# Encoder kernel: where weight sums are copied and added, when norm rows are loaded, and how far the down projection splits ahead

## The chip, the cores and the metric

The kernel runs on one core of one Trainium2 chip. The metric is the device time of one execution in microseconds; the time before is 1022.74 us, the median of 3 runs (1021.55 to 1024.2).

## What is computed

An encoder layer over two batches of 512 tokens with 1024 channels, in float32. After an input layer norm come windowed attention and a Fourier mixing path, an output projection, a residual layer norm, and a gated feed-forward block with a width-3 convolution. What the change touches is the end:

```python
def layer_norm(x, g, b):
    mu = mean(x); var = mean((x - mu) ** 2)
    return (x - mu) * rsqrt(var + EPS) * g + b

def conv_ffn(x, w_up, conv_w, conv_b, w_down):
    h = conv3(x @ w_up, conv_w) + conv_b          # 1024 -> 2 * 2816
    a, u = split(h, 2)
    return (gelu(a) * u) @ w_down                 # 2816 -> 1024

x = layer_norm(ALPHA * x + mix, ln1_g, ln1_b)
x = layer_norm(ALPHA * x + conv_ffn(x, w_up, conv_w, conv_b, w_down), ln2_g, ln2_b)
```

## The kernel before

Each engine has its own instruction list, written out by hand, and waits on semaphores. A float32 matmul is made of three matmuls on reduced operands: each operand is split into a high part (a copy by ACT, helper line 1862) and a low part (the difference, by DVE, helper line 1267, or 1700 where the sign turns). TensorE therefore needs ACT's and then DVE's split of each operand.

*Stages.* Input norm and projections, attention and Fourier mixing (to about 230 us), output projection and `x1` (the normed residual), up projection over 22 feature tiles `v` (about 310 to 764 us), down projection, final norm.

*Up projection.* For each tile of 128 features, SP loads `w_raw` two tiles ahead (`load_up`, two DMAs), DVE forms sums of weight blocks, both engines split, TensorE does seven products. DVE's `gate` writes `gated`, and SP's `store_gated` stores it to DRAM; behind each odd tile it also stores `gsum`, four row sums. The first 18 tiles (`PAIRED`) form 9 pairs (`QUADS`).

*Weight sums.* The down projection of these 18 tiles works on 2 x 2 blocks in seven products instead of eight (`PRODUCTS`), so it needs four sums of blocks of `w_down`, kept in `ts_scratch` in DRAM. SP copies blocks there (`start_weight_sum`, twelve copies of 768 KB, one behind each `load_up` of tiles 2 to 13); when four copies of a chunk have landed, POOL adds other blocks onto them with accumulating DMAs (`weight_row_sums`, lines 748 to 755, four for each chunk of three pairs, 768 KB each): two side by side, then a third, then a fourth, each waiting for the one before.

*Down projection.* 21 steps: three chunks of seven products (`STEPS`). Step `n` uses operand slot `n % 5`. SP's `load_step(n)` loads `ga_raw` and `db_raw` once step `n - 5` is done. ACT's `step_high` and DVE's `step_low` split them two steps ahead of TensorE. A step is four tiles (`t`) of nine matmuls, into four PSUM banks; two sets of banks alternate, so a step waits until the banks of step `n - 2` are taken. Steps 0, 2, 3 and 6 are taken by ACT (`take_step`, a copy to `part_sum`), the others by DVE (`add_step`, line 1802, added to `part_sum`).

*The first residual.* SP reloads `x1` into `acc` (eight DMAs, 512 KB each, line 589), then the norm rows `gain_bc` and `bias_bc` (lines 590, 591). ACT scales both rows after its work of step 0, and everything else of ACT is queued behind that. POOL then does `acc * gain + bias` in sixteen operations (`residual`, lines 725 and 727), and, once the last steps are taken, `acc + part_sum` in eight (line 772).

*The end.* The four unpaired feature tiles are multiplied last (`down_last`, 16 groups of 12 matmuls), from splits `last_high` and `last_low`. DVE adds each group to `acc` (`add_last`, line 1810), then statistics (1270), the centring and the scaling (1835, 1842); SP stores the result.

Of the kernel before, what the change touches and what calls it, by code (L numbers as in the profile page):

```python
# [13 lines left out]
P = 128  # L14
# [155 lines left out]
def build(nc, x_prompt, x_sample, ln_in_g, ln_in_b, rel_table, w_in, attn_sink, w_fourier, g_attn,  # L170
# [172 lines left out]
    with ExitStack() as ctx:  # L343
# [17 lines left out]
        ts_copy = [sem(f"ts_copy{c}") for c in range(QUADS // CHUNK)]  # L361
# [62 lines left out]
        def _(sp):  # L424
# [69 lines left out]

            sp.wait_ge(proj_ps, 2 * TILES)
            sp.wait_ge(ss_ps, 1)
            load_wo(0)
            sp.wait_ge(logit_done, GRP * UNITS)
# [34 lines left out]
            def start_weight_sum(j):  # L533

                c, i = divmod(j, 4)
                src = (quarter[B11], quarter[B22], b12, quarter[B21])[i]
                sp.dma_start(ts_dram[i, :, quads(c), :], src[:, quads(c), :]).then_inc(ts_copy[c], 16)

            def load_step(n):
                c, i = divmod(n, 7)  # L540
                a, w, s = PRODUCTS[i][0], PRODUCTS[i][1], n % SLOTS
                if i == 0:
                    for e in range(2):
                        sp.wait_ge(g_out[e], 32 * CHUNK * (c + 1))
                    sp.wait_ge(gs_out, 16 * CHUNK * (c + 1))
                    sp.wait_ge(ts_sum, 64 * (QUADS // CHUNK))
# [18 lines left out]
            for v in range(FT):  # L565
                if v < PLAIN:
                    sp.wait_ge(c_ps, 4 * v + 4)
                    load_up(v + 2)
                elif v + 2 < FT:
                    sp.wait_ge(p_ps[3], v + 1 - PLAIN)  # L570
                    load_up(v + 2)
                    if v - PLAIN < 12:
                        start_weight_sum(v - PLAIN)
                elif v + 2 == FT:
                    sp.wait_ge(p_ps[3], v + 1 - PLAIN)
                    sp.wait_ge(p_ps[1], FT - PLAIN)
# [13 lines left out]
            sp.dma_start(gain_bc[:], ln1_g.partition_broadcast(P)).then_inc(gb_in, 16)  # L590
            sp.dma_start(bias_bc[:], ln1_b.partition_broadcast(P)).then_inc(gb_in, 16)
# [23 lines left out]
        def _(pool):  # L615
# [126 lines left out]
            def weight_row_sums(c, part):  # L742


                k, w = [ts_dram[i, :, quads(c), :] for i in range(4)], quads(c)
                if part == 0:
                    pool.wait_ge(ts_copy[c], 64)
                    pool.dma_start(k[0], b12[:, w, :], accum_op=ALU.add).then_inc(ts_sum, 16)  # L748
                    pool.dma_start(k[2], quarter[B22][:, w, :], accum_op=ALU.add).then_inc(ts_sum, 16)
                elif part == 1:  # L750
                    pool.wait_ge(ts_sum, 64 * c + 32)
                    pool.dma_start(k[1], k[0], accum_op=ALU.add).then_inc(ts_sum, 16)
                else:
                    pool.wait_ge(ts_sum, 64 * c + 48)
                    pool.dma_start(k[3], k[1], accum_op=ALU.add).then_inc(ts_sum, 16)

            for c in range(QUADS // CHUNK):
                for part in range(3):
                    weight_row_sums(c, part)
# [5 lines left out]
            for t in range(TT):  # L765

                pool.wait_ge(x0_ready, TT + t + 1)
                if t < TB:
                    pool.wait_ge(dn_dve, taken(STEPS - 2, t)[1])
                else:  # L770
                    pool.wait_ge(dn_dve, taken(STEPS - 1, t - TB)[1])
                pool.tensor_tensor(acc[:, t, :], acc[:, t, :], part_sum[:, t, :], ALU.add).then_inc(x0_ready, 1)
# [490 lines left out]
        def _(dve):  # L1263
# [455 lines left out]
            def up_tail(v):  # L1719
# [17 lines left out]
                sum_c12(v)  # L1737
                gate(v, 0)
# [6 lines left out]
                if v + 2 < FT:  # L1745
                    low_a11(v + 2)
                    sum_c11(v + 1)
                    if v % 2 and v < PAIRED:
                        row_sums(v)
                elif v + 2 == FT:  # L1750
                    step_low(0, 0)
                    step_low(0, 1)
                else:
                    step_low(1, 1)
# [57 lines left out]
            lows = [(0, 0), (0, 1), (1, 0), (1, 1), (2, 0), (2, 1), (3, 0), (3, 1)]  # L1812
            for n in range(STEPS):
                for t in range(TB):
                    if not by_act(n):
                        add_step(n, t)
                    if t % 2 and n + 2 < STEPS:
                        step_low(n + 2, t // 2)
                    elif n + 2 == STEPS and t == 3:
                        last_low(0, 0)  # L1820
                        last_low(0, 1)
                    elif n + 1 == STEPS:
                        if t == 1:
                            for j, w in lows[2:5]:
                                last_low(j, w)
                        elif t == 3:
                            for j, w in lows[5:8]:
                                last_low(j, w)
# [30 lines left out]
        def _(act):  # L1859
# [336 lines left out]
            def up_tail(v):  # L2196
# [11 lines left out]
                centre(v, up_bank(v, 0), 1, 0)  # L2208
                gelu(v, 0)
# [11 lines left out]
                else:  # L2221
                    step_high(1, 1)
# [40 lines left out]
            for n in range(STEPS):  # L2263
                for t in range(TB):
                    if by_act(n):
                        take_step(n, t)
                    if t % 2 and n + 2 < STEPS:
                        step_high(n + 2, t // 2)
                if n == 0:
# [57 lines left out]
```

## Time and profile before

| | |
|---|---|
| time, median of 3 runs | 1022.74 us |
| profiled execution | 1024.54 us |
| its span, first to last instruction | 1022.7 us |
| TensorE matmul busy | 971.3 us, 95% |
| DVE busy | 794.6 us, 78% |
| ACT busy | 487.6 us, 48% |
| POOL busy | 243.9 us, 24% |
| mean granted clock of TensorE | 0.981 |
| DMA moved | 142.21 MB |

The profile comes from one execution. Times in the trace are microseconds from the span's start. A wait is put down to the producer whose signal ended it. PE is TensorE, SPq and POOLq are the issuing of DMAs by these engines.

### The profile page before, as it was taken

The numbers are of one execution on the slowest core, as the hardware profiler recorded it, in microseconds if no ns is written. First come the engines' busy times: TensorE is split into PE (matmuls) and PEld (weight loads), VectorE is DVE, ScalarE is ACT, GpSimd is POOL, SyncE is SP. The second block draws the span as 40 slices with busy tenths as digits, with TensorE's granted clock in tenths as the row PEclk, the third lists the DMA queues.
The fourth block names the chain that finished last, engine by engine and source line by source line (L and its number), as shares of the span: only waits on it lengthen the run. The fifth ranks groups of instructions, "written<-read, shape, count | busy, mean of one in ns | idle before, by whom it ended". The sixth has DMA issues, their size and how long they took to land. (4 is left out here: it accounts for less than half of the span.)

```text
span 1022.7 us, 12252 instructions
## 1 busy us (share of the span) xinstructions
PE 971.3 (95%) x4506; PEld 806.9 (79%) x4506; DVE 794.6 (78%) x1156; ACT 487.6 (48%) x748; POOL 243.9 (24%) x222
## 2 busy tenths in 40 slices
PE   7999999999999999999999999999998499999596
PEld 5888888998888788887888788788886388888385
DVE  6664667886776899988887887888783689776988
ACT  5574667986113755444444544544542545333000
POOL 2400336784930000001001001000000795001722
PEclk9999999999999999999999999999999699999799
DMA  8334131009032114349539639524258555754012
GB/s 301 94 99 128 42 104 42 1 3 324 15 133 92 54 52 144 134 154 226 165 115 242 168 124 232 139 93 144 83 201 319 224 195 201 244 199 158 8 62 103
DMA packets 108891, 142.21 MB, mean 139 GB/s; under 512 B 20779, under 2 KB 71935, under 8 KB 108832
## 3 DMA queue, kind: packets, MB, share of 16 engines
q1 hardware_dynamic: 104352, 129.82, 38.2%
q0 software_dynamic: 3264, 9.44, 5.3%
q10 hardware_dynamic: 1216, 2.17, 0.7%
q8 instruction: 36, 0.59, 0.2%
q14 instruction: 23, 0.19, 0.1%
HBM read 112.32 MB, written 47.97 MB: 157 GB/s over the span
## 5 line engine op out<-in xcount | busy, mean ns | idle before, releaser
L780 PE MATMUL ps<-db_hi,ga_hi 128*128 128x512 f32 x252 | 99.2, 394 | 16.9 <-DVE db_lo L1267 16.9
L781 PE MATMUL ps<-db_lo,ga_hi 128*128 128x512 f32 x252 | 98.8, 392 | 0.0
L782 PE MATMUL ps<-db_hi,ga_lo 128*128 128x512 f32 x252 | 98.8, 392 | 0.0
L780 PE MATMUL ps<-x1h,wa_hi 128*128 128x512 f32 x192 | 76.6, 399 | 6.8 <-DVE w_lo L1267 6.8
L781 PE MATMUL ps<-x1l,wa_hi 128*128 128x512 f32 x192 | 75.5, 393 | 0.0
L782 PE MATMUL ps<-x1h,w_lo 128*128 128x512 f32 x192 | 75.3, 392 | 0.0
L2159 ACT ACTIVATE hc<-U,taps 128x512 f32<-128x512 f32 x60 | 48.7, 813 | 54.1 <-DVE U L1649 41.5
L725 POOL TENSOR_TENSOR acc<-acc,gain_bc 128x1024 f32<-128x1024 f32 x12 | 37.9, 3154 | 152.9 <-ACT bias_bc L1862 152.9
L780 PEld LDWEIGHTS ps<-db_hi,ga_hi 128*128 128x128 f32 x252 | 47.8, 190 | 27.6 <-issue 17.7
L1267 DVE TENSOR_TENSOR ga_lo<-ga_raw,ga_hi 128x1536 fp32r<-128x1536 f32 x21 | 45.2, 2153 | 26.4 <-ACT ga_hi L1862 26.4
L1802 DVE TENSOR_TENSOR part_sum<-part_sum,ps 128x512 f32<-128x512 f32 x68 | 45.3, 681 | 24.6 <-PE ps L782 24.6
L2164 ACT ACTIVATE hc<-hc 128x512 f32<-128x512 f32 x44 | 27.8, 633 | 71.1 <-DVE hc L1666 71.1
L748 POOL DMA_DIRECT2D ts_scratch<-in_w_down x3 | 4.0, 1333 | 238.0 <-DMA ts_scratch<-in_w_down 238.0
L1862 ACT ACTIVATE wa_hi<-w_raw 128x1024 fp32r<-128x1024 f32 x44 | 46.4, 1062 | 26.0 <-DVE w_raw L1567 16.6
L781 PEld LDWEIGHTS ps<-db_lo,ga_hi 128*128 128x128 f32 x252 | 47.9, 190 | 10.0
L782 PEld LDWEIGHTS ps<-db_hi,ga_lo 128*128 128x128 f32 x252 | 47.8, 189 | 10.0
L1267 DVE TENSOR_TENSOR w_lo<-w_raw,wa_hi 128x512 fp32r<-128x512 f32 (+1 forms) x64 | 54.8, 884 | 0.0
L1862 ACT ACTIVATE ga_hi<-ga_raw 128x1536 fp32r<-128x1536 f32 x21 | 31.2, 1484 | 48.8 <-DMA db_raw<-in_w_down 24.2
L780 PEld LDWEIGHTS ps<-x1h,wa_hi 128*128 128x128 f32 x192 | 36.3, 189 | 15.5 <-DVE w_lo L1267 8.1
L1662 DVE SCALAR_TENSOR_TENSOR hc<-U,taps,hc 128x511 f32<-128x511 f32 x60 | 43.2, 748 | 5.7 <-ACT hc L2159 5.7
L1862 ACT ACTIVATE U<-ps 128x512 f32<-128x512 f32 x60 | 35.5, 591 | 24.9 <-PE ps L782 24.9
L634 POOL TENSOR_TENSOR rstd<-ve,half_neg 128x1 f32<-128x1 f32 x20 | 22.2, 1112 | 94.0 <-DVE ve L1280 94.0
(318 smaller groups left out, 2961.9 us busy)
## 6 DMA issues: line engine op xcount, KB each, us to landing
w_raw<-in_w_up SPq DMA_DIRECT2D x44, 512.0 KB, 5.2
ga_raw<-gs_scratch SPq DMA_DIRECT2D x21, 768.0 KB, 4.7
gs_scratch<-gsum SPq DMA_DIRECT2D x9, 1024.0 KB, 4.7
ts_scratch<-in_w_down SPq DMA_DIRECT2D x12, 768.0 KB, 6.9
db_raw<-ts_scratch SPq DMA_DIRECT2D x12, 768.0 KB, 6.1
db_raw<-in_w_down SPq DMA_DIRECT2D x9, 768.0 KB, 6.8
gs_scratch<-gated SPq DMA_DIRECT2D x9, 512.0 KB
ts_scratch<-in_w_down POOLq DMA_DIRECT2D x6, 768.0 KB, 12.3
```

Source lines behind the costliest of these rows:

```text
L634: pool.tensor_tensor(rstd[:, t:t + 1], ve[:, t:t + 1], half_neg[:, 0:1], ALU.pow).then_inc(rstd_ready, 1)
L725: chain.mark(pool.tensor_tensor(dst, dst, gain_bc[:], ALU.mult))
L748: pool.dma_start(k[0], b12[:, w, :], accum_op=ALU.add).then_inc(ts_sum, 16)
L780: pe.matmul(out, whi, xhi, start=start, stop=False, skip_group_check=onto)
L781: pe.matmul(out, whi, xlo, start=False, stop=False, skip_group_check=onto)
L782: return pe.matmul(out, wlo, xhi, start=False, stop=stop, skip_group_check=onto)
L1267: dve.tensor_tensor(out, full, f32(hi), ALU.subtract).then_inc(done, 1)
L1662: chain.mark(dve.scalar_tensor_tensor(out=hc[:, part, b, 1:SEQ], in0=src[:, 0:SEQ - 1], scalar=tap(v, part, 0), in1=hc[:, part, b, 1:SEQ], ...
L1802: dve.tensor_tensor(dst, dst, ps[:, DOWN_BANKS[n % 2][t], :], ALU.add if sign > 0 else ALU.subtract).then_inc(dn_dve, 1)
L1862: ins = act.activation(out, in_, ACT.Copy, scale=scale) if scale != 1.0 else act.activation(out, in_, ACT.Copy)
L2159: act.activation(hc[:, part, b, :], src, ACT.Identity, bias=taps[:, 1, col + 2 * FT:col + 2 * FT + 1], scale=taps[:, 0, col + 2 * FT:col + ...
L2164: act.activation(hc[:, 0, b, :], hc[:, 0, b, :], ACT.Gelu).then_inc(gelu_done, 1)
```

## The change

The edits, in the order of the diff:

- `ts_copy` becomes one semaphore. SP issues all twelve copies in the attention stage, behind `load_wo(0)` and ahead of its wait for the logits, and none in the up projection.
- POOL's accumulating DMAs become 36 of 256 KB: for each pair two behind the gates of its even tile and two, one after the other, behind those of its odd tile (`g_ready`).
- SP loads `gain_bc` and `bias_bc` for the first residual in the last tile of the up projection, behind `load_step(2)`, ahead of the last store and of the `x1` loads. ACT scales them after its splits of step 1's loop pass, not of step 0's.
- Splits of the down projection run three steps ahead; the second half of step 1 is split before the last gates and gelus.
- Steps 14 to 20 add straight into `acc`, on DVE. POOL adds the `part_sum` of the first two chunks to `acc` in sixteen half-width operations as soon as each quarter is complete (steps 8, 11, 12, 13). DVE's adds of steps 14 to 20 wait for these; its `add_last` waits for DVE's own adds only.
- The splits of the last four tiles are spread over steps 18 to 20.

```diff
@@ SP, attention stage
             load_wo(0)
+            for j in range(4 * (QUADS // CHUNK)):
+                start_weight_sum(j)
             sp.wait_ge(logit_done, GRP * UNITS)
@@ SP, up projection
                     load_up(v + 2)
-                    if v - PLAIN < 12:
-                        start_weight_sum(v - PLAIN)
...
                     load_step(2)
+                    sp.wait_ge(gs_out, 16 * QUADS)
+                    sp.dma_start(gain_bc[:], ln1_g.partition_broadcast(P)).then_inc(gb_in, 16)
+                    sp.dma_start(bias_bc[:], ln1_b.partition_broadcast(P)).then_inc(gb_in, 16)
                 store_gated(v)
...
                 sp.dma_start(acc[:, t, :], x1_dram[t]).then_inc(x_in[t], 16)
-            sp.dma_start(gain_bc[:], ln1_g.partition_broadcast(P)).then_inc(gb_in, 16)
-            sp.dma_start(bias_bc[:], ln1_b.partition_broadcast(P)).then_inc(gb_in, 16)
@@ POOL
+            def weight_row_sums(v):
+                q, k = v // 2, [ts_dram[i, :, v // 2, :] for i in range(4)]
+                pool.wait_ge(g_ready, 2 * v + 2)
+                if v % 2 == 0:
+                    pool.dma_start(k[0], b12[:, q, :], accum_op=ALU.add).then_inc(ts_sum, 16)
+                    pool.dma_start(k[2], quarter[B22][:, q, :], accum_op=ALU.add).then_inc(ts_sum, 16)
+                else:
+                    pool.wait_ge(ts_sum, 64 * q + 32)
                     pool.dma_start(k[1], k[0], accum_op=ALU.add).then_inc(ts_sum, 16)
+                    pool.wait_ge(ts_sum, 64 * q + 48)
                     pool.dma_start(k[3], k[1], accum_op=ALU.add).then_inc(ts_sum, 16)
...
-            for t in range(TT):
-                pool.wait_ge(x0_ready, TT + t + 1)
...
-                pool.tensor_tensor(acc[:, t, :], acc[:, t, :], part_sum[:, t, :], ALU.add).then_inc(x0_ready, 1)
+            for n in (8, 11, 12, 13):
+                first, half, _ = TARGETS[n - 7]
+                cols = slice(half * 512, half * 512 + 512)
+                for t in range(TB):
+                    pool.wait_ge(x0_ready, TT + first + t + 1)
+                    pool.wait_ge(dn_dve, taken(n, t)[1])
+                    pool.tensor_tensor(acc[:, first + t, cols], acc[:, first + t, cols], part_sum[:, first + t, cols], ALU.add).then_inc(x0_ready, 1)
@@ DVE (ACT's lists change in the same way)
                 sum_c12(v)
+                if v + 1 == FT:
+                    step_low(1, 1)
                 gate(v, 0)
...
-                dst = part_sum[:, first + t, half * 512:(half + 1) * 512]
+                dst = (part_sum if n < 14 else acc)[:, first + t, half * 512:(half + 1) * 512]
...
+                if n >= 14:
+                    dve.wait_ge(x0_ready, 2 * TT + {(0, 0): 0, (4, 1): 4, (0, 1): 8, (4, 0): 12}[first, half] + t + 1)
...
-                if half == 0:
-                    dve.wait_ge(x0_ready, 2 * TT + t + 1)
+                if t < TB:
+                    dve.wait_ge(dn_dve, taken((15, 19)[half], t)[1])
+                else:
+                    dve.wait_ge(dn_dve, taken((20, 18)[half], t - TB)[1])
...
+            lows = {(18, 1): (0,), (18, 3): (1,), (19, 1): (2,), (19, 3): (3, 4), (20, 1): (5, 6), (20, 2): (7,)}
             for n in range(STEPS):
                 for t in range(TB):
                     if not by_act(n):
                         add_step(n, t)
...
+                    if n == 0:
+                        step_low(2 + t // 2, t % 2)
+                    elif t % 2 and n + 3 < STEPS:
+                        step_low(n + 3, t // 2)
+                    for k in lows.get((n, t), ()):
+                        last_low(k // 2, k % 2)
@@ ACT
-                if n == 0:
+                if n == 1:
                     act.wait_ge(gb_in, 64)
                     copy(gain_bc[:], gain_bc[:], gb_ready, ALPHA)
```

## Rows read from the trace of the kernel before

**Rows 1.** Waits of TensorE, all: line, releaser, us in total, times, longest.
```profile
PE ps L780 <- DVE db_lo L1267: 16.9, 2, 15.9
PE ps L780 <- DVE d_lo L1267: 11.6, 3, 5.2
PE ps L780 <- DVE w_lo L1267: 6.8, 3, 2.4
```
**Rows 2.** Timeline of SP's DMA issues, down stage: start, duration, line, tile.
```profile
841.22 0.32 SPq L549 DMA_DIRECT2D ga_raw<-gs_scratch  x1
...
849.38 0.32 SPq L549 DMA_DIRECT2D ga_raw<-gs_scratch  x1
```
**Rows 3.** Busy time by stretch: PE, PEld, DVE, ACT, POOL; granted clock, DMA share, GB/s.
```profile
772.60:806.20 33.60, 16.72 (x73) 13.46 (x73) 12.29 (x10) 13.29 (x15) 7.86 (x3) 0.81 1.02 395
...
976.40:1022.70 46.30, 37.99 (x168) 31.14 (x166) 42.46 (x64) 0.00 (x0) 11.64 (x8) 0.96 0.23 91
```
**Rows 4.** Timelines of PE and ACT around the first stall; brackets: idle before, releaser.
```profile
806.21 0.77 PE L780 MATMUL ps<-db_hi,ga_hi 128*128 128x512 f32 x1 [15.90 <-DVE db_lo L1267]
...
796.18 1.06 ACT L1862 ACTIVATE gain_bc<-gain_bc 128x1024 f32<-128x1024 f32 x1 [19.72 <-DMA bias_bc<-in_ln_b]
```
**Rows 5.** Timelines of PE, ACT, POOL and DVE around the second stall.
```profile
961.30 0.79 PE L780 MATMUL ps<-d_hi,g_hi 128*128 128x512 f32 x1 [5.20 <-DVE d_lo L1267]
...
949.81 1.04 ACT L1862 ACTIVATE d_hi<-d_raw 128x1024 fp32r<-128x1024 f32 x1
...
942.24 10.44 POOL L772 TENSOR_TENSOR acc<-acc,part_sum 128x1024 f32<-128x1024 f32 x4 [85.00 <-DVE part_sum L1802]
...
950.36 3.41 DVE L1267 TENSOR_TENSOR d_lo<-d_raw,d_hi 128x1024 fp32r<-128x1024 f32 x1
...
961.17 1.21 DVE L1267 TENSOR_TENSOR g_lo<-g_raw,g_hi 128x1024 fp32r<-128x1024 f32 x1
...
976.35 0.69 DVE L1810 TENSOR_TENSOR acc<-ps,acc 128x512 f32<-128x512 f32 x1 [2.15 <-PE ps L782]
```
**Rows 6.** Busy time by stretch, up projection; columns as in rows 3.
```profile
480.00:500.00 20.00, 17.66 (x71) 14.09 (x71) 15.52 (x21) 8.84 (x11) 0.81 (x1) 0.91 0.73 178
500.00:520.00 20.00, 20.00 (x90) 16.57 (x89) 17.74 (x25) 9.08 (x12) 0.00 (x0) 1.00 0.55 185
```
**Rows 7.** Landing of w_raw: loads issued from 453 us, and from 472 us.
```profile
DMA to landing us min/median/max: 4.1/4.7/5.3
...
DMA to landing us min/median/max: 7.6/8.2/8.9
```
**Rows 8.** Timelines of POOL's accumulating DMAs and of SP's issues, same place.
```profile
487.45 0.81 POOL L755 DMA_DIRECT2D ts_scratch<-ts_scratch  x1 [8.30 <-DMA ts_scratch<-ts_scratch]
...
462.28 0.40 SPq L529 DMA_DIRECT2D gs_scratch<-gated  x1
...
472.32 2.58 SPq L513 DMA_DIRECT2D w_raw<-in_w_up  x2
```
**Rows 9.** Waits of SP's queue: the one for the logits in the attention stage.
```profile
SPq L493 <- DVE negm L1470: 63.1, 1, 63.1
```
**Rows 10.** Busy time by stretch, attention stage and behind it; columns as in rows 3.
```profile
170.00:180.00 10.00, 9.71 (x65) 8.81 (x65) 7.93 (x26) 8.96 (x27) 7.42 (x13) 1.00 0.01 2
...
230.00:240.00 10.00, 10.00 (x53) 8.44 (x52) 5.16 (x9) 5.40 (x10) 4.45 (x8) 1.00 1.04 316
```
**Rows 11.** Issue of load 5's second half on SP, and its landing.
```profile
783.43 1.05 SPq L551 DMA_DIRECT2D db_raw<-in_w_down  x1
...
DMA to landing us min/median/max: 16.6/16.6/16.6
```
**Rows 12.** Timeline of DVE: low parts beside POOL with adds between, back to back, alone.
```profile
803.35 2.72 DVE L1267 TENSOR_TENSOR db_lo<-db_raw,db_hi 128x1536 fp32r<-128x1536 f32 x1
...
809.83 3.95 DVE L1700 SCALAR_TENSOR_TENSOR db_lo<-db_raw,db_hi 128x1536 fp32r<-128x1536 f32 x1
...
839.15 1.80 DVE L1267 TENSOR_TENSOR ga_lo<-ga_raw,ga_hi 128x1536 fp32r<-128x1536 f32 x1 [2.07 <-ACT ga_hi L1862]
```

More of the change, by code:

```diff
@@ L360, in build @@
         gs_sum, ts_sum = sem("gs_sum"), sem("ts_sum")
-        ts_copy = [sem(f"ts_copy{c}") for c in range(QUADS // CHUNK)]
+        ts_copy = sem("ts_copy")
         step_in = [sem(f"step_in{s}") for s in range(SLOTS)]
@@ L493, in load_wo, with start_weight_sum @@
                         sp.dma_start(wor[p][kv * HD:(kv + 1) * HD], rows).then_inc(wo_in[p], 16)
+            def start_weight_sum(j):
+                c, i = divmod(j, 4)
+                src = (quarter[B11], quarter[B22], b12, quarter[B21])[i]
+                sp.dma_start(ts_dram[i, :, quads(c), :], src[:, quads(c), :]).then_inc(ts_copy, 16)
             sp.wait_ge(proj_ps, 2 * TILES)
@@ L531, in store_gated @@
                     sp.dma_start(gs_dram[S1:S4 + 1, :, q, :].rearrange("i p n -> p i n"), gsum[:]).then_inc(gs_out, 16)
[L533 to L537, printed above, removed]
             def load_step(n):
@@ L545, in load_step @@
                     sp.wait_ge(gs_out, 16 * CHUNK * (c + 1))
-                    sp.wait_ge(ts_sum, 64 * (QUADS // CHUNK))
+                    sp.wait_ge(ts_sum, 64 * QUADS)
                 if n >= SLOTS:
@@ L740, in _ @@
                 ln_rstd(t, TT)
[L742 to L751, printed above, removed]
+            def weight_row_sums(v):
[6 more added lines that the diff above has]
+                    pool.wait_ge(ts_sum, 64 * q + 32)
                     pool.dma_start(k[1], k[0], accum_op=ALU.add).then_inc(ts_sum, 16)
-                else:
-                    pool.wait_ge(ts_sum, 64 * c + 48)
+                    pool.wait_ge(ts_sum, 64 * q + 48)
                     pool.dma_start(k[3], k[1], accum_op=ALU.add).then_inc(ts_sum, 16)
-            for c in range(QUADS // CHUNK):
-                for part in range(3):
-                    weight_row_sums(c, part)
+            pool.wait_ge(ts_copy, 64 * (QUADS // CHUNK))
+            for v in range(PAIRED):
+                weight_row_sums(v)
             pool.wait_ge(gb_ready, 3)
@@ L764, in _ @@
                 residual(acc[:, t, :])
-            for t in range(TT):
-                pool.wait_ge(x0_ready, TT + t + 1)
[L768 to L771, printed above, removed]
-                pool.tensor_tensor(acc[:, t, :], acc[:, t, :], part_sum[:, t, :], ALU.add).then_inc(x0_ready, 1)
+            for n in (8, 11, 12, 13):
[5 more added lines that the diff above has]
+                    pool.tensor_tensor(acc[:, first + t, cols], acc[:, first + t, cols], part_sum[:, first + t, cols], ALU.add).then_inc(x0_ready, 1)
             for t in range(TT):
@@ L1752, in up_tail @@
                     step_low(0, 1)
-                else:
-                    step_low(1, 1)
             for j in range(4):
@@ L1807, in add_last @@
                 dve.wait_ge(dn_ps, 4 * STEPS + i + 1)
-                if half == 0:
-                    dve.wait_ge(x0_ready, 2 * TT + t + 1)
+                if t < TB:
+                    dve.wait_ge(dn_dve, taken((15, 19)[half], t)[1])
+                else:
+                    dve.wait_ge(dn_dve, taken((20, 18)[half], t - TB)[1])
                 dve.tensor_tensor(acc[:, t, cols], ps[:, last_bank(i), :], acc[:, t, cols], ALU.add).then_inc(dn_dve, 1)
-            lows = [(0, 0), (0, 1), (1, 0), (1, 1), (2, 0), (2, 1), (3, 0), (3, 1)]
+            lows = {(18, 1): (0,), (18, 3): (1,), (19, 1): (2,), (19, 3): (3, 4), (20, 1): (5, 6), (20, 2): (7,)}
             for n in range(STEPS):
@@ L1816, in _ @@
                         add_step(n, t)
[L1817 to L1828, printed above, removed]
+                    if n == 0:
[4 more added lines that the diff above has]
+                        last_low(k // 2, k % 2)
             def pieces(t):
@@ L2208, in up_tail @@
                 centre(v, up_bank(v, 0), 1, 0)
+                if v + 1 == FT:
+                    step_high(1, 1)
                 gelu(v, 0)
@@ L2220, in up_tail @@
                     step_high(0, 1)
-                else:
-                    step_high(1, 1)
             for k in range(3):
@@ L2266, in _ @@
                         take_step(n, t)
-                    if t % 2 and n + 2 < STEPS:
-                        step_high(n + 2, t // 2)
-                if n == 0:
+                    if n == 0:
+                        step_high(2 + t // 2, t % 2)
+                    elif t % 2 and n + 3 < STEPS:
+                        step_high(n + 3, t // 2)
+                if n == 1:
                     act.wait_ge(gb_in, 64)
```

## The prediction

> **What bounds the kernel now.** I read TensorE's waits first: it is busy 95% of the span, so what can be won is where it stands still. Three producers hold it up for 35.3 us: `db_lo` (16.9), `d_lo` (11.6) and `w_lo` (6.8) [rows 1]. Each is DVE's second half of an operand split, late for a reason of its own. To price them I compare what TensorE would have taken. In the down projection the loads go out at the end of a step, and two issues in a row stand 8.16 us apart [rows 2]; a step is 36 matmuls, so one costs 0.2267 us at full clock.
>
> *First stall.* TensorE stands 15.90 us before step 3 [rows 4], in a stretch with 0.81 of full clock, full DMA engines (share 1.02) and 395 GB/s [rows 3]. The cause is on ACT: it waits 19.72 us for the norm row `bias_bc`, and only then takes up the work behind it, which includes step 3's splits [rows 4]. The norm rows are queued on SP behind eight 512 KB loads of `x1`.
>
> *Second stall.* Before the last four feature blocks TensorE waits three times for `d_lo`, 5.20 us the longest. A last split of 1.21 us alone takes 3.41 on DVE while POOL adds `part_sum` to `acc` [rows 5]. Behind it DVE sets the pace to the end: in 976.40 to 1022.70 it is busy 42.46 of 46.30 us, TensorE 37.99 [rows 3].
>
> *Third.* In the up projection three stalls of up to 2.4 us [rows 1] stand where `w_raw` took 8.2 us to land and not 4.7 [rows 7], because POOL's 768 KB accumulating DMAs are in the way.
>
> **The change part by part.**
>
> *A. Small accumulates.* The first of three such places has 71 matmuls in 20 us against 90 in its neighbour [rows 6]; the other two have 78 and 79. That is 19 + 12 + 11 = 42 matmuls, 9.5 us. The load landed 3.5 us later and the stall was at most 2.4, so some 1.1 us of slack covers each `w_raw`. Now a piece has a third of the bytes and starts when `gated` is done, which SP's store shows at 462.28; the next `w_raw` load is issued at 472.32, 10.0 us later. A wide accumulate took 8.3 us of waiting and 0.8 of issue, 9.1 [rows 8]; by bytes a piece takes 3.0. An odd tile has two in series, 6.1 us, beside 1.57 MB of stores (4.0 us at the 395 GB/s of rows 3): 10.1 if nothing overlaps, the size of the gap, with 1.1 of slack behind it. An even tile has two side by side and a smaller store. I take the whole 9.5 us as won; bounds 4 and 9.5. The Trainium skill (DMA: Bandwidth & Descriptors, "Anatomy of one DMA" and "Bandwidth") gives a DMA that POOL issues some 2.0 us fixed plus bytes / 436e3 us, and advises 1 MiB or more, which speaks against 36 small ones. By it a piece is estimated at 2.6 us and the pair at 5.2, which changes little; but it makes a wide one 3.8 us where the trace has 9.1, so a fixed part could be larger too (rival 4).
>
> *B. Copies in the attention stage.* SP waits 63.1 us there for the logits [rows 9], and the copies go in ahead of that wait. One is 0.79 MB; at the 316 GB/s of a full queue [rows 10] that is 2.5 us, and twelve are 30, so they are through in half of SP's wait and the `wo` loads behind it aren't late. The DMA share there is 0.01. That a full queue disturbs nobody is seen a little later, where the share is 1.04 and TensorE busy 10.00 of 10 us [rows 10]. Cost 0; bounds 0 and 3. The copies' old places show no stall of their own, so nothing is won there.
>
> *C. Norm rows sooner, and ACT's order.* The rows are now issued behind load 2 and ahead of the last store and the `x1` loads; they land some ten us before ACT asks. Then the 15.9 us wait is gone, and I ask what is late next. I write the order out by hand with step 0 starting at 0 (764.40 in the old trace; loads, splits and steps in us from there). Step 1's `db_lo` is split ahead of the last gates: ACT is idle there, DVE is not, so the last gate, its store and loads 3 and 4 move back by 1.5, and in return the 1.0 us before step 1 (16.9 less 15.9 [rows 1]) goes. Load 3 lands at 16.6 and load 4 at 20.5. Load 5 landed at 783.43 + 16.6 = 800.0 [rows 11], 35.6 after the start; less 2.6 for the 1.05 MB of norm rows that were ahead of it, plus 1.5, it lands at 34.5. ACT, with 1.47 a split, has step 3 by 20.0, step 4 by 23.4, the norm rows by 25.3, step 2's first two banks by 26.4. It then waits for load 5, has its first half at 36.0 and empties the third bank by 36.6. TensorE wants that bank at 4.5 steps, 36.7: it just goes through. Step 5 starts at 40.8. Its two low parts on DVE come back to back beside POOL's residual. Such a split took 3.95, one with adds around it 2.72, and one with POOL out of the way 1.80 [rows 12]. From 36.0, a first one of 1.8 to 3.95 and a second of 3.95 end at 41.8 to 43.9, so step 5 starts 1.0 to 3.1 us late; step 6 has the same pair close behind and may lose 1 more. I take 3.0 us of new stall, bounds 0.5 and 6. The Trainium skill (SBUF — State Buffer, on the shared port pair) says that DVE and GpSimd take an exclusive lock for a whole instruction; by that rule, the trace agrees: beside POOL the split costs 2.15 us more.
>
> Steps 0 to 20 took from 764.40 to 955.4 (961.30 less the wait of 5.20 and three matmuls of 0.23 [rows 5]), 191.0 us, where 21 x 8.16 = 171.4 would do. Of the 19.6 us between, 19.6 - 3.0 = 16.6 are won.
>
> *D. Last splits ahead, third chunk straight into `acc`.* Behind step 17 no step split is left for DVE, so steps 18 to 20 hold the adds (0.69 each) and eight last splits (1.21 each). The latest high part comes from ACT at 949.81 + 1.04 [rows 5], 3.6 us into step 20. The last `d_lo` is placed behind the third add of step 20, about 8.0 into it, and ends at 9.2; TensorE wants it at 8.16 + 9 x 0.2267 = 10.2. POOL's eight wide adds (2.6 us each, 10.44 for four [rows 5]) become sixteen half ones behind steps 8 to 13. POOL is through with the residual at about 25 + 16 x 3.8 = 86 and needs about 1.4 for each half add; DVE's new wait on it begins with step 14 at about 118, behind which DVE's splits of step 17 and all later adds are queued, and isn't late. So the second add into `acc` comes 24 matmuls and 0.3 us after step 20, at 955.4 + 5.4 + 0.3 = 961.1 instead of 976.35 [rows 5]: 15.2 us won; bounds 11 (a pair of splits late) and 15.2. The 46.3 us behind it stay.
>
> **Sum.** 9.5 + 16.6 + 15.2 = 41.3 us. The profiled execution's span 1022.7 becomes 981.4 and its time 1024.54 becomes 983.2. That time is 1.8 above the median of the runs, 1022.74, which becomes 981.4. Forecast 982.
>
> **Rivals.**
> 1. *The wait becomes one for load 5.* 4.2 MB of `x1` are still ahead of it, and ACT, three ahead, now stands before it with step 2's banks not yet emptied. For: the margin above is 0.1 us. A load that is 4 us late costs 4, and some 2 more by the low clock (the first place in A lost 4.3 us with a wait of 2.4): 988. Against: less is ahead of it than before. Chance 0.19; 985 to 991.
> 2. *The accumulates still meet `w_raw`* in a few tiles. Then A gives nothing: 991. Against: the 10 us gap. Chance 0.10.
> 3. *The tail keeps its waits* as DVE or POOL runs late after step 5 and never catches up; D gives nothing: 997. Against: with POOL done, splits take 1.8 us again and a step leaves DVE idle. Chance 0.04.
> 4. *Slower than before.* An accumulate's 9.1 us is fixed and not by bytes. Two in series from 462.5 then run to 480.7, and every `w_raw` load from 472.3 meets one. At 4.3 us a tile, 18 tiles lose 77: 981.4 + 9.5 + 77 = 1068. It decides from the 8th such tile on, as (41.3 - 9.5) / 4.3 = 7.4. Against: nothing at all of a 768 KB transfer would have to depend on its size. Chance 0.03, and 0.01 for a milder one that just cancels the gain.
> 5. *It doesn't do what it says:* the norm rows gate ACT as before: 998. Against: they are issued before the `x1` loads in the code. Chance 0.03.
>
> **How the numbers follow.** The forecast case has 0.60, with a range of its own of 977 to 986. The range takes in rivals 1 and 2 and the bounds of A to D: 976 to 993. About 0.3%, 3 us, is what a measurement of this kernel can tell from no change. Faster 0.96, within 0.3% 0.01, slower 0.03.
>
> **What the new profile should show.** No `db_lo` wait over 4 us; if there is one it stands before step 4's third tile or at step 5. ACT's longest wait in the down stage is for load 5. No `d_lo` wait, and no `acc` add of POOL after step 14. `w_raw` lands in under 6.5 us in all tiles, and every 20 us of the up stage have 88 to 90 matmuls. A DMA share near 1 for some 30 us in the attention stage, with TensorE as busy as before. A `w_lo` wait at every second tile would prove me wrong on A, a stall before the last blocks on D, and one over 6 us at steps 3 to 7 on C.

## The result and the profile after

The changed kernel takes 982.37 us (median of 4 runs, 981.47 to 983.99); the kernel before took 1022.16 in the runs beside it. The ratio is 0.9609, with a 95% interval of 0.9589 to 0.9629: 40.0 us less, between 37.9 and 42.0. The forecast was 982, its range 976 to 993.

The profiled execution took 981.47 us with a span of 979.6. The first four waits of TensorE after the change (line, releaser, us in total, times, longest):

```profile
PE ps L786 <- DMA rows_a<-in_ln_in_b: 4.9, 1, 4.9
PE ps L781 <- DVE db_lo L1268: 1.0, 1, 1.0
PE ps L804 <- ACT acc L1872: 1.0, 1, 1.0
PE ps L781 <- ACT part_sum L1861: 0.3, 1, 0.3
```

Of the three producers in rows 1, `d_lo` and `w_lo` are gone and `db_lo` has 1.0 us left of 16.9; with the `part_sum` wait 1.3 us remain. What was there at the kernel's start (4.9) is there still. The busy time by stretch answers rows 6 and, behind the dots, rows 10, the two stretches in which the copies run:

```profile
480.00:500.00 20.00, 20.00 (x90) 16.58 (x89) 16.47 (x24) 10.71 (x14) 1.90 (x3) 1.00 0.41 93
...
170.00:180.00 10.00, 9.75 (x66) 8.82 (x64) 7.92 (x25) 9.00 (x26) 8.11 (x15) 1.00 1.00 331
180.00:190.00 10.00, 10.00 (x61) 9.21 (x60) 8.70 (x24) 8.73 (x24) 7.55 (x13) 1.00 1.03 334
```

The up projection has its 90 matmuls in 20 us, and the attention stage runs beside a full queue (share 1.00 and 1.03) as it did beside an empty one: 66 matmuls and 9.75 us where rows 10 have 65 and 9.71. The down stage, timelines of ACT and TensorE:

```profile
778.05 1.04 ACT L1861 ACTIVATE gain_bc<-gain_bc 128x1024 f32<-128x1024 f32 x1
...
789.45 1.49 ACT L1861 ACTIVATE ga_hi<-ga_raw 128x1536 fp32r<-128x1536 f32 x1 [8.45 <-DMA db_raw<-in_w_down]
...
791.48 0.51 PE L781 MATMUL ps<-db_hi,ga_hi 128*128 128x512 f32 x1 [0.32 <-ACT part_sum L1861]
796.87 0.47 PE L781 MATMUL ps<-db_hi,ga_hi 128*128 128x512 f32 x1 [0.98 <-DVE db_lo L1268]
```

ACT takes up the norm rows without waiting (rows 4: 19.72 us), and its longest wait there, 8.45 us, is now for load 5. The end, timelines of POOL and DVE, which answer rows 5:

```profile
854.47 26.00 POOL L773 TENSOR_TENSOR acc<-acc,part_sum 128x512 f32<-128x512 f32 x12 [5.32 <-DVE part_sum L1805]
...
927.26 1.22 DVE L1268 TENSOR_TENSOR d_lo<-d_raw,d_hi 128x1024 fp32r<-128x1024 f32 x1
...
930.65 0.69 DVE L1815 TENSOR_TENSOR acc<-ps,acc 128x512 f32<-128x512 f32 x1 [1.57 <-issue]
...
933.31 0.69 DVE L1815 TENSOR_TENSOR acc<-ps,acc 128x512 f32<-128x512 f32 x1 [1.24 <-PE ps L783]
```

POOL's adds end at 880.5 and the last split takes 1.22 us alone.

**Where the 43.1 us of span went.** The first matmul of step 0, TensorE's timeline:

```profile
754.27 0.39 PE L781 MATMUL ps<-db_hi,ga_hi 128*128 128x512 f32 x1
```

Step 0 starts at 754.3 where it started at 764.4: 10.1 us. Step 20 ends at 927.7 (930.65 less twelve matmuls and 0.3), so the 21 steps take 173.4 instead of 191.0: 17.6. From there to the second add into `acc` it is 5.6 us instead of 20.9: 15.3. The tail behind it is 46.3 as before. The span shrank by more than the 40.0 us of the ratio: the profiled execution before stood 1.8 us above its kernel's median, the one after 0.9 below.

### The profile page after: what moved, and what is told of

The parts are those of the page before. It is cut to its first block, busy times and chain, and to the rows that moved or that the text cites. A ratio compares the mean times of both kernels' runs of the same rounds, so it can differ in the third digit from the quotient of the medians.

```text
span 979.6 us, 12310 instructions
## 1 busy us (share of the span) xinstructions
PE 963.2 (98%) x4506; PEld 803.8 (82%) x4506; DVE 788.2 (80%) x1156; ACT 488.4 (50%) x748; POOL 275.3 (28%) x254
## 4 chain that ended last, share of the span: by engine, by line
PE 88%; DVE 6%; DMA 2%; ACT 2%; issue 2%; POOL 0%; DVEq 0%; SPq 0%; ACTq 0%; POOLq 0%
PE ps L781 28%; PE ps L783 28%; PE ps L782 28%; DMA db_raw<-in_w_down 2%; DVE bn L1271 1%; DVE acc L1834 1%; PE ps L995 1%; DVE acc L1815 1%; PE ps L1124 1%; DVE prob L1471 1%; DVE pTl L1268 1%; ACT prob L2038 1%; PE ps L816 1%; ACT pTh L1861 0%; DMA acc<-in_x_prompt 0%
## 5 line engine op out<-in xcount | busy, mean ns | idle before, releaser
L726 POOL TENSOR_TENSOR acc<-acc,gain_bc 128x1024 f32<-128x1024 f32 x12 | 37.9, 3160 | 83.8 <-ACT bias_bc L1861 83.8
L1268 DVE TENSOR_TENSOR ga_lo<-ga_raw,ga_hi 128x1536 fp32r<-128x1536 f32 x21 | 47.9, 2283 | 16.7 <-ACT ga_hi L1861 16.7
L753 POOL DMA_DIRECT2D ts_scratch<-ts_scratch x9 | 7.3, 811 | 155.3 <-DVE gated L1677 155.3
L749 POOL DMA_DIRECT2D ts_scratch<-in_w_down x9 | 7.6, 842 | 142.8 <-DVE gated L1679 142.8
L1663 DVE SCALAR_TENSOR_TENSOR hc<-U,taps,hc 128x511 f32<-128x511 f32 x60 | 43.1, 746 | 5.5 <-ACT hc L2158 5.5
L1667 DVE SCALAR_TENSOR_TENSOR hc<-U,taps,hc 128x511 f32<-128x511 f32 x60 | 43.3, 749 | 1.4
```

The costliest lines, as they stand in the source:

```text
L726: chain.mark(pool.tensor_tensor(dst, dst, gain_bc[:], ALU.mult))
L1268: dve.tensor_tensor(out, full, f32(hi), ALU.subtract).then_inc(done, 1)
L1663: chain.mark(dve.scalar_tensor_tensor(out=hc[:, part, b, 1:SEQ], in0=src[:, 0:SEQ - 1], scalar=tap(v, part, 0), in1=hc[:, part, b, 1:SEQ], ...
L1667: dve.scalar_tensor_tensor(out=hc[:, part, b, 0:SEQ - 1], in0=src[:, 1:SEQ], scalar=tap(v, part, 1), in1=hc[:, part, b, 0:SEQ - 1], op0=AL ...
```

## Experiments

Differences to the changed kernel are differences of the ratios to the kernel before, times 1022.7. Each ratio has an interval of about 0.2 points to either side, so a difference is good to some 3 us; smaller ones rest on the waits. The profiled executions give a second measure, from the first matmul of step 0 to the end of the span: 258.3 us before, 225.3 in the changed kernel; e1 238.8, e3 242.4, e4 226.6, e5 228.9, e7 228.2, e8 234.5, e9 244.3, e10 223.4, e11 241.4, e12 229.7. It leaves out the stages ahead, which scatter: with the new sums step 0 starts anywhere from 754.3 to 755.7 us. It is one execution of each kernel, and is called the down time below.

**e1, the norm rows put back.**

```diff
-                    sp.wait_ge(gs_out, 16 * QUADS)
-                    sp.dma_start(gain_bc[:], ...)      # and bias_bc, in the last tile
...
                 sp.dma_start(acc[:, t, :], x1_dram[t]).then_inc(x_in[t], 16)
+            sp.dma_start(gain_bc[:], ...)              # and bias_bc
...
-                if n == 1:
+                if n == 0:
                     act.wait_ge(gb_in, 64)
```

> The changed kernel with the norm rows put back behind the x1 loads and ACT's scaling of them back at the end of step 0's pass; the splits stay three steps ahead. Theory (the rows gate ACT, but with three steps ahead step 3's splits are already done when ACT stops, so the stall is at step 4 and smaller): rows land about 33 us after the start of step 0, step 4's splits end about 40 to 42 where TensorE wants them at 32.7; with the low clock behind it the time is 9 to 11 us over the changed kernel's 982.4, 991 to 994. Rival (the place of the rows is the whole cure, depth nothing): the old stall of 16 to 18 us is back, 998 to 1001. Rival (the depth alone covers the wait): 982 to 984.

Measured 994.19 us, ratio 0.9707 (0.9691 to 0.9724): 10.0 us more (13.5 in the down time). The size is the theory's, the place isn't. Timelines of TensorE, ACT and DVE:

```profile
795.98 0.80 PE L780 MATMUL ps<-db_hi,ga_hi 128*128 128x512 f32 x1 [12.54 <-DVE part_sum L1804]
...
789.28 1.06 ACT L1860 ACTIVATE gain_bc<-gain_bc 128x1024 f32<-128x1024 f32 x1 [13.94 <-DMA bias_bc<-in_ln_b]
...
792.69 2.65 DVE L1267 TENSOR_TENSOR ga_lo<-ga_raw,ga_hi 128x1536 fp32r<-128x1536 f32 x1 [14.36 <-ACT ga_hi L1860]
795.25 1.27 DVE L1804 TENSOR_TENSOR part_sum<-part_sum,ps 128x512 f32<-128x512 f32 x2
```

TensorE doesn't wait for step 4's splits but for a bank, in the middle of step 3: DVE's list has step 4's first low part ahead of the adds that empty step 1's last two banks. ACT stops for the norm rows, DVE for ACT's high part, and TensorE for the add queued behind it. Both lists run in order, so here the late load reached TensorE through a bank before it could through an operand.

**e9, the norm rows put back and splits two steps ahead.** The edits are those of e1 and e4 together.

> The changed kernel with both the norm rows put back (SP's place and ACT's place) and the splits two steps ahead. Alone the rows cost 0.98 points of the time and the depth 0.04. Theory (with two ahead ACT's stop lies in front of step 3's splits, so the whole old stall is back; with three ahead it only lay in front of step 4's): a db_lo wait of 14 to 16 us before step 3, 15 to 18 us over the changed kernel, a ratio of 0.976 to 0.979 to the kernel before. Rival (the two parts simply add up): 10 to 11 us, a ratio of 0.971 to 0.972.

Measured 1002.00 us, ratio 0.9781 (0.9759 to 0.9804): 17.6 us more (18.9 in the down time). The time is the theory's, the wait is longer than it said, 18.8 us, and it is the old one, for `db_lo` before step 3:

```profile
798.70 0.76 PE L780 MATMUL ps<-db_hi,ga_hi 128*128 128x512 f32 x1 [18.80 <-DVE db_lo L1267]
```

The parts do not add up (10.0 and 0.4 would be 10.4): depth is worth nothing that can be measured once the rows are early, and some 7 us while they are late (5.4 in the down time, 18.9 less 13.5).

**e4, splits two steps ahead.**

```diff
-                    if n == 0:
-                        step_low(2 + t // 2, t % 2)
-                    elif t % 2 and n + 3 < STEPS:
-                        step_low(n + 3, t // 2)
+                    if t % 2 and n + 2 < STEPS:
+                        step_low(n + 2, t // 2)        # ACT's step_high alike
...
-            lows = {(18, 1): (0,), (18, 3): (1,), (19, 1): (2,), ...}
+            lows = {(18, 3): (0, 1), (19, 1): (2,), ...}
```

> The changed kernel with splits two steps ahead again in steps 0 to 20 (the two last splits of step 18 come behind its fourth tile so that the order of signals holds). Theory (once the norm rows are out of the way, the limit at steps 4 and 5 is the landing of load 5 and DVE beside POOL, which the depth does not move): 0 to 2 us more, 982 to 985. Rival (the depth is what carries TensorE over the full queue): 8 us more or worse, over 990.

Measured 984.24 us, ratio 0.9613 (0.9596 to 0.9630): 0.4 us more, no difference that can be measured. The waits show a small one:

```profile
798.52 0.47 PE L781 MATMUL ps<-db_hi,ga_hi 128*128 128x512 f32 x1 [3.05 <-DVE db_lo L1268]
```

It is 3.05 us before step 5 against 1.3 in two waits, and the down time is 1.3 us longer. The third step of depth buys at most 1.8 us here.

**e5, only SP's loads of the norm rows put back behind `x1`;** ACT scales them at the end of step 1's pass.

> The changed kernel with only SP's two norm row loads put back behind the x1 loads; ACT still scales them at the end of step 1's pass. This puts 1.05 MB more ahead of load 5 and makes ACT wait for the rows until about 33 us after the start of step 0, just before it empties step 2's banks. Theory (a margin of nothing at step 4, so each us that load 5 is late costs about one us): load 5 lands 2.6 us later, TensorE's waits in steps 4 to 6 rise from 1.3 us to 4 to 6, 3 to 5 us more than the changed kernel, 985 to 988, and up to 2 more if the clock falls. Rival (there is slack that I did not see): 982 to 983.

Measured 985.89 us, ratio 0.9628 (0.9608 to 0.9649): 1.9 us more by the ratios, within the scatter of the 3 to 5 expected; the span of the profiled run is 4.3 longer (983.9), its down time 3.6. TensorE waits 3.3 us, in one piece. Step 0 starts at 755.0 there, so the wait, from 787.8 on, is at the first tile of step 4, for the first bank of step 2. Timelines of TensorE and ACT:

```profile
791.04 0.50 PE L780 MATMUL ps<-db_hi,ga_hi 128*128 128x512 f32 x1 [3.27 <-ACT part_sum L1860]
...
788.51 1.06 ACT L1860 ACTIVATE gain_bc<-gain_bc 128x1024 f32<-128x1024 f32 x1 [9.95 <-DMA bias_bc<-in_ln_b]
```

The size is near the theory's, the mechanism isn't. Load 5 does come some 2 us later (ACT takes it up at 792.47, 37.5 after the start of step 0, against 35.2), but TensorE already stands by then: ACT has waited for `bias_bc` with step 2's banks still full. By the time that ACT has load 5's first half and empties the third bank (793.86), TensorE is late enough not to wait for it. So the run says nothing on the slack for load 5; e10 does. What it shows is the price of the rows alone: the same late rows cost 2 to 4 us when ACT asks for them behind step 4's splits, and 17.6 in front of step 3's (e9). Of the 3.6, 2.0 are waits and about 1.6 the clock: in the 4 us behind the wait TensorE has a granted clock of 0.61 and 11 matmuls, where 17 to 19 are usual.

**e10, load 5 ahead of the eight `x1` loads.**

```diff
+            load_step(5)
             for t in range(TT):
                 sp.dma_start(acc[:, t, :], x1_dram[t]).then_inc(x_in[t], 16)
-            for n in range(SLOTS, STEPS):
+            for n in range(SLOTS + 1, STEPS):
```

> The changed kernel with the loads of step 5 issued ahead of the eight x1 loads, nothing else. Theory (load 5 behind 4.2 MB of x1 is what is left of the stall): load 5 lands some 10 us sooner, TensorE's two waits in steps 4 to 6, 1.3 us in all, go; 1 us less than the changed kernel, a ratio of 0.959 to 0.961, hardly to be told from none by the time, so the waits decide. Rival (DVE beside POOL makes the wait, whenever the load lands): a db_lo wait of 1 us or more stays or moves to step 6.

Measured 980.41 us, ratio 0.9573 (0.9553 to 0.9593). TensorE has no wait left between 175 us and the end. Its waits, all but the last two (0.3 us or less):

```profile
PE ps L787 <- DMA rows_a<-in_ln_in_b: 4.9, 1, 4.9
PE ps L805 <- ACT acc L1873: 1.3, 2, 0.9
PE ps L846 <- ACT xh L1894: 0.3, 1, 0.3
```

Load 5 was what was left of the stall: with it early, DVE's low parts of steps 5 and 6 take 3.6 to 4.0 us beside POOL, and nobody waits for them. The down time is 2.0 us shorter and leaves 171.4 us for the 21 steps, their time at full clock. The rest of the ratio's difference (0.36 points, 3.7 us) isn't shown, as the intervals overlap. Its runs are 980.16 to 980.89, the lowest median of all kernels tried.

**e11, the kernel before with only the norm rows moved.** The edits are those of e1 read backwards, on the kernel before; the new loads stand in the same place as in the change.

> The kernel before with only the norm rows moved as in the change (SP's loads in the last tile of the up projection, ACT's scaling at the end of step 1's pass); splits two steps ahead, sums and tail as before. Theory (this part alone cures the first stall and leaves the other two): the wait before step 3 goes, 1 to 3.5 us of db_lo waits appear at steps 4 to 6, w_lo (6.8) and d_lo (11.6) stay; 14 to 17 us less, a ratio of 0.983 to 0.986 to the kernel before. Rival (the depth was needed too): under 10 us, a ratio over 0.990.

Measured 1005.81 us, ratio 0.9823 (0.9798 to 0.9848): 18.1 us less than before, a little over the 14 to 17 expected, and 16.9 less in the down time. The other two producers are as in rows 1:

```profile
PE ps L781 <- DVE d_lo L1268: 11.7, 3, 5.2
PE ps L781 <- DVE w_lo L1268: 6.0, 3, 2.1
...
PE ps L781 <- DVE db_lo L1268: 1.5, 2, 1.1
```

Two moved loads and one moved pair of copies are worth nearly half of the whole change. What I had priced too high are the new waits, 1 to 3.5 us at steps 4 to 6: here they are 0.4 (the other 1.1 is the old one before step 1). With an interval of 2.6 us to either side the ratio doesn't tell 18.1 from 17.

**e3, the tail put back.** The third chunk into `part_sum`, POOL's eight wide adds behind it, the last splits behind steps 19 and 20.

```diff
-                dst = (part_sum if n < 14 else acc)[:, first + t, half * 512:(half + 1) * 512]
+                dst = part_sum[:, first + t, half * 512:(half + 1) * 512]
...
-            lows = {(18, 1): (0,), (18, 3): (1,), (19, 1): (2,), (19, 3): (3, 4), (20, 1): (5, 6), (20, 2): (7,)}
+            lows = {(19, 3): (0, 1), (20, 1): (2, 3, 4), (20, 3): (5, 6, 7)}
```

> The changed kernel with the third chunk into part_sum, POOL's eight wide adds at the end and the last splits where they were. Theory: three d_lo waits of 11 to 12 us in all and low clock behind them, 15.2 us more, 996 to 999. Rival (the tail gained in the change because DVE arrived less behind at step 18, not by this part): under 8 us more, below 990.

Measured 999.40 us, ratio 0.9760 (0.9745 to 0.9775): 15.4 us more (17.0 in the down time), with 11.4 us of `d_lo` waits. The next two kernels divide it.

**e7, only the places of the last splits put back** (the second edit of e3), POOL's adds early.

> The changed kernel with only the last splits put back to their old places (two behind step 19, three and three in step 20); POOL's adds stay early. Theory (POOL's port use made most of the second stall): uncontended splits of 1.21 us end 13.5 us after the start of step 20 where the last is wanted at 10.2; 3 to 5 us more, 985 to 988. Rival (the places alone made the stall): 12 us or more, over 994.

Measured 986.25 us, ratio 0.9632 (0.9611 to 0.9653): 2.4 us more (2.8 in the down time), just under the 3 to 5 expected and within the scatter. Two short waits:

```profile
930.88 0.50 PE L781 MATMUL ps<-d_hi,g_hi 128*128 128x512 f32 x1 [1.08 <-DVE d_lo L1268]
933.15 0.50 PE L781 MATMUL ps<-d_hi,g_hi 128*128 128x512 f32 x1 [1.31 <-DVE d_lo L1268]
```

**e8, only POOL's adds late** (the first edit of e3 and the adds that belong to it), the splits in their new places.

> The changed kernel with the last splits in their new places but the third chunk into part_sum and POOL's eight wide adds at the end as before. Theory: the splits of steps 19 and 20 take about 3.3 us each beside POOL, the last ends about 18.8 us into step 20 where it is wanted at 10.2, with low clock behind it 9 to 11 us more, 991 to 994. Rival (the new places are enough): 982 to 984.

Measured 993.70 us, ratio 0.9701 (0.9680 to 0.9722): 9.4 us more (9.2 in the down time). TensorE, DVE and POOL:

```profile
932.54 0.50 PE L782 MATMUL ps<-d_hi,g_hi 128*128 128x512 f32 x1 [2.01 <-DVE d_lo L1269]
937.57 0.80 PE L782 MATMUL ps<-d_hi,g_hi 128*128 128x512 f32 x1 [4.08 <-DVE d_lo L1269]
...
932.40 3.38 DVE L1269 TENSOR_TENSOR g_lo<-g_raw,g_hi 128x1024 fp32r<-128x1024 f32 x1
935.71 0.67 DVE L1804 TENSOR_TENSOR part_sum<-part_sum,ps 128x512 f32<-128x512 f32 x1
936.31 1.21 DVE L1269 TENSOR_TENSOR d_lo<-d_raw,d_hi 128x1024 fp32r<-128x1024 f32 x1
...
931.36 3.35 POOL L774 TENSOR_TENSOR acc<-acc,part_sum 128x1024 f32<-128x1024 f32 x1
936.53 3.22 POOL L774 TENSOR_TENSOR acc<-acc,part_sum 128x1024 f32<-128x1024 f32 x1 [1.82 <-DVE part_sum L1804]
```

POOL's part is the larger, some three to four times. A split of this size takes 3.38 us when it starts while an add of POOL is running (932.40, the add ends at 934.71), and 1.21 when POOL is idle as it starts (936.31); POOL's next add, begun at 936.53 during that split, is then the one that takes longer, 3.22 us against 2.3 for the add behind it. An add from PSUM takes 0.67 in both places. The two undone singly make 11.8 of the 15.4 us (12.0 of 17.0 in the down time); the rest shows only with both undone, or is scatter.

**e2, the weight sums put back.** Twelve copies behind the loads of tiles 2 to 13, accumulates of 768 KB.

```diff
             load_wo(0)
-            for j in range(4 * (QUADS // CHUNK)):
-                start_weight_sum(j)
...
                     load_up(v + 2)
+                    if v - PLAIN < 12:
+                        start_weight_sum(v - PLAIN)
```

> The changed kernel with the weight sums as before: twelve copies behind the loads of tiles 2 to 13, accumulates of 768 KB. Theory (these DMAs delay three w_raw loads, and nothing else hangs on them): three w_lo waits of 2.0 to 2.4 us in the up projection, 9.5 us more than the changed kernel, 991 to 993. Rival (those stalls were made by something else in the stage and the copies are free): 982 to 984.

Measured 992.01 us, ratio 0.9687 (0.9671 to 0.9704): 8.0 us more, 10.4 in the span. Three `w_lo` waits of 3.04, 1.40 and 2.06 us, 6.5 in all; step 0 starts 10.9 us later.

**e6, early copies, wide accumulates** behind the gates of tiles 5, 9 and 13.

```diff
-                pool.wait_ge(g_ready, 2 * v + 2)
+                if part == 0:
+                    pool.wait_ge(g_ready, 8 * c + 12)
+                    pool.dma_start(k[0], b12[:, w, :], accum_op=ALU.add)    # w: three pairs at once
```

> The changed kernel with the copies early, in the attention stage, but with accumulates of 768 KB, started behind the gates of tiles 5, 9 and 13, where they ran before. Theory (the size of the accumulates delays w_raw, not the copies): the three w_lo waits are back, w_raw lands in 7.5 to 9 us there, 7 to 9.5 us more, 989 to 992. Rival (the copies in the same queue did it, or needed to be there too): no wait or under 1 us each, 982 to 984.

Measured 989.60 us, ratio 0.9663 (0.9643 to 0.9682): 5.5 us more, less than the 7 to 9.5 expected, though step 0 starts 7.1 us later. The three waits are back, and `w_raw` lands late again behind tile 5. Waits, then that landing:

```profile
PE ps L783 <- DVE w_lo L1270: 5.9, 3, 2.5
...
DMA to landing us min/median/max: 8.0/8.5/9.0
```

The copies were out of the queue and it didn't help: the accumulates, wide as they are, make the waits. What the copies add to them, 2.5 us by the ratios, is within the scatter.

**e12, small accumulates, late copies.** POOL waits for a chunk's four copies before its first piece.

```diff
+                if v % 6 == 0:
+                    pool.wait_ge(ts_copy[v // 6], 64)
                 pool.wait_ge(g_ready, 2 * v + 2)
```

> The changed kernel with the small accumulates kept but the twelve copies back behind the loads of tiles 2 to 13; POOL waits for the four copies of a chunk before the chunk's first piece. The first pair's pieces can't start before about 461 us then, and twelve of them (two side by side and two in series for each of three pairs, about 5.4 us each) run on end for some 50 us, over two or three w_raw loads. Theory (what hurts is how many bytes of accumulate are ahead of a load: one piece is 1.5 to 3 us of queue where about 1.1 us of slack stands, a wide one or two are 4 and more): w_raw lands in up to 6 to 7.5 us, a few w_lo waits of under 1.3 us each, 0 to 3 us over the changed kernel, a ratio of 0.961 to 0.964. Rival (any accumulate beside a load makes the full stall, and only the pacing by the gates saved the changed kernel): w_lo waits of 2 us or more at several tiles, 8 us or more, a ratio over 0.968.

Measured 990.12 us, ratio 0.9656 (0.9615 to 0.9696), 4.8 us more: between the two, and a wide interval. The waits speak for neither as written. In the profiled execution, the slowest of the four (994.98), step 0 starts 9.2 us later than in the changed kernel, which is between the 7.1 of e6 and the 10.9 of e2; its down time is 4.4 us longer too, with a `db_lo` wait of 2.88 us and a `part_sum` wait of 1.26, and why is open. Timelines of TensorE and POOL; then the landing of the two halves of `w_raw` issued at 472.8, and of those issued at 491.8:

```profile
505.00 0.50 PE L782 MATMUL ps<-x1h,wa_hi 128*128 128x512 f32 x1 [2.35 <-DVE w_lo L1269]
565.78 0.50 PE L782 MATMUL ps<-x1h,wa_hi 128*128 128x512 f32 x1 [1.77 <-DVE w_lo L1269]
...
470.52 0.81 POOL L755 DMA_DIRECT2D ts_scratch<-ts_scratch  x1 [6.62 <-DMA ts_scratch<-in_w_down]
474.86 0.81 POOL L757 DMA_DIRECT2D ts_scratch<-ts_scratch  x1 [3.53 <-DMA ts_scratch<-ts_scratch]
...
491.54 1.13 POOL L751 DMA_DIRECT2D ts_scratch<-in_w_down  x1
492.07 1.44 POOL L752 DMA_DIRECT2D ts_scratch<-in_w_down  x1
...
DMA to landing us min/median/max: 5.0/5.5/6.1
...
DMA to landing us min/median/max: 5.1/7.0/8.9
```

The load at 472.8 has one single piece just ahead of it and lands in at most 6.1 us, without a wait. The load at 491.8 meets a single one (issued at 491.0) and the pair above: its first half lands in 5.1 us, its second in 8.9, and TensorE stands 2.35 us, as long as beside a wide one (2.50 in e6, where the halves land in 8.0 and 9.0). So a third of the bytes isn't enough: small pieces bunched around a load made a wait of the full length at two tiles. The change needs both, pieces that fit the gap (e6) and their start behind the gates, which puts them there (e12); the early copies make that pacing possible. A copy behind a load does no harm by itself: the loads issued at 434.7, 453.7 and 515.1 each have one behind them and no piece beside them, and land in at most 5.3 us. What copy and pair do together, against the pair alone, was not tried.

## Why the prediction was right

**A, small accumulates.** Forecast 9.5 us, measured 8.0 by time (e2) and 10.1 at the start of step 0. That start is 754.3 to 755.7 in the nine kernels with the new sums and 762.0 (e11), 764.4 and 765.2 (e2) with the old ones, so the part is worth 6 to 11 us. The cause is shown by e6. The reason I gave for it being free was partly wrong. I took the price of a piece by bytes, 3.0 us; POOL and SP in the changed kernel show more:

```profile
466.98 0.81 POOL L755 DMA_DIRECT2D ts_scratch<-ts_scratch  x1 [4.58 <-DMA ts_scratch<-ts_scratch]
...
471.55 1.00 SPq L521 DMA_DIRECT2D w_raw<-in_w_up  x2
```

A piece is 4.58 + 0.81 = 5.4 us (5.0 to 5.4 at the other odd tiles). With 9.1 for three times the bytes (rows 8) that makes, as an estimate, some 3.5 us fixed and 1.9 by bytes (nearer 4 and 1.4 with the 7.5 to 8.3 us of e6's wide ones), so rival 4 had the mechanism half right. Two in series from 461.6 end near 472, as the load is issued, so the 10.0 us gap was filled and `w_raw` landed in at most 5.5 us. By the prediction's own sum, in which nothing overlaps, two pieces and the stores would have been 10.8 + 4.0 = 14.8 us, more than the gap and its slack of 1.1. That they fitted is due to the overlap with the stores, on which the prediction had not counted; that A gave all it could is in part luck. The Trainium skill's fit (DMA: Bandwidth & Descriptors, "Anatomy of one DMA") has a fixed part too, 2.0 us, and gives 2.6 for a piece; the trace is twice that, and the measurement decides. e12 shows how near it was: with the pieces elsewhere the waits are back.

**B, copies in the attention stage.** Forecast 0, with 30 us of full queue. The share is 1.00 and 1.03 where rows 10 had 0.01, down to 0.01 again by 200, and TensorE is as busy as before. Right. No run has the early copies alone; that they cost nothing rests on these stretches, and on e6, which is not slower than e2.

**C, norm rows and depth.** Forecast 16.6, measured 17.6. Load 5 was expected at 34.5 us after the start of step 0; ACT takes it up at 789.45, which is 35.2. The wait at step 4's third tile was expected at 36.7 with no margin; it is there, 0.32 us, and ends at 791.48, 37.2 after the start. The term that was off is the new stall, 3.0 forecast; the 21 steps took 2.0 us over the 171.4 of full speed, 1.3 of it waits. The first low part took 1.9 us and the second 3.4, at the short end of 1.8 to 3.95 for the first, because an operation of POOL was just ending as it started (790.98; POOL's ends at 791.22), and step 6 lost nothing. That the depth isn't what cured the wait, which the prediction left open by costing both in one part, is shown by e4 and e11.

**D, the tail.** Forecast 15.2, measured 15.3, and 15.4 undone (e3). The last `d_lo` was expected to end 9.2 us into step 20 and ends at 927.26 + 1.22, 9.0 in. One price was wrong without harm: a half-width add of POOL was put at 1.4 us and takes 2.2 to 2.9 (26.00 for twelve above, 11.40 for the four ahead of them), so POOL adds until 880.5, in step 15, where the prediction wanted none behind step 14. DVE waited for none of them, and POOL is done 39 us before step 20 starts. e7 and e8 show how it divides.

**The sum.** 41.3 forecast, 43.1 in the span, 40.0 by the ratio, which is good to 2 us: that 982 was hit to less than one is luck. Parts undone singly cost 8.0 + 10.0 + 0.4 + 15.4 = 33.8; with rows and depth undone together 8.0 + 17.6 + 15.4 = 41.0. Each term is good to some 3 us; the one coupling that shows is between those two.

**The rivals.** The first was the near one: e10 shows that load 5 does set the pace at steps 4 and 5, at 2.0 us and not at 6. The second, accumulates still in the way, would have been true with another pacing (e12). The third and fifth did not happen, nor did the slower case.

## What to carry to other kernels

When an engine works off a list in order, ask of each wait in it what stands behind, through two engines if need be: the same late norm rows made waits of 18.8, 12.5 or 3.3 us, by what ACT had split before it asked for them. In a queue that is full, order loads by when they are wanted, not by what belongs together; and place background transfers in the gap behind a load, by their measured time: cutting them smaller made them fit the gap here, and was not enough where they ran beside a load. Move GpSimd's work over SBUF away from a stretch in which VectorE's splits are on the path.

## What the runs showed of the hardware that I had not expected

An accumulating DRAM-to-DRAM transfer issued by POOL, from its issue to the signal of its landing, takes 5.0 to 5.4 us for 256 KB in the changed kernel, and for 768 KB 7.8 to 9.8 at the three places before the change (9.1 in rows 8) and 7.5 to 8.3 in e6: three times the bytes in less than twice the time. Small ones bunched around a 1 MB load held up its second half as long as wide ones (8.9 us to landing against 9.0), and its first half not at all (5.1 against 8.0).

How long TensorE stood did not decide whether its granted clock (full is 2.4 GHz, the low level 1.2) fell afterwards. These are the 4 us from the end of a wait of 3.05 us in e4, and of one of 3.27 us in e5:

```profile
798.52:802.52 4.00, 4.00 (x18) 3.33 (x19) 4.00 (x4) 2.87 (x2) 3.92 (x2) 1.00 1.02 409
...
791.04:795.04 4.00, 4.00 (x11) 3.19 (x12) 1.05 (x1) 3.01 (x5) 3.92 (x2) 0.61 1.03 421
```

The clock also fell behind waits of 1.77 and 2.35 us in e12 (0.66 and 0.58), 2.34 before the change (0.61) and 3.04 in e2 (0.63), and stayed at 1.00 behind 2.44 us before the change and 2.50 in e6. What divides them stays open. It matters for reading small differences: a stall of the same length costs about 1.6 us more where the clock falls (11 matmuls in 4 us, not 18).
